# Two blocks in one chip: a delta rule's start reordered between VectorE and GpSimd, a band added by one matmul a head, a gain row fetched through DRAM

## The reference, cut to what matters

```python
def rmsnorm(x, g):
    xf = x.astype(jnp.float32)
    y = xf * lax.rsqrt(jnp.mean(xf * xf, axis=-1, keepdims=True) + EPS)
    return (y * g.astype(jnp.float32)).astype(x.dtype)
...
    return rmsnorm(h, final_norm)          # first model's end, (256, 1024) times a row of 1024 gains
...
# gated delta rule, 6 heads, chunks of 64 tokens (reference form)
lower = jnp.where(strict, jnp.einsum("bhncd,bhnkd->bhnck", kb, k) * decay, 0.0)
sol = lax.linalg.triangular_solve(lower, rhs, left_side=True, lower=True, unit_diagonal=True)
...
# sliding window attention, 12 heads, window 128
s = jnp.where(mask[None, :, None, None], s, -jnp.inf)
m = jnp.maximum(jnp.max(s, axis=-1, keepdims=True), sink)
p = jnp.exp(s - m)
p = (p / (jnp.sum(p, axis=-1, keepdims=True) + jnp.exp(sink - m))).astype(v.dtype)
```

## Time and profile before

| | |
|---|---|
| time, median of 3 runs | 1551.87 us (1551.78 to 1552.45) |
| the profiled execution's own time | 1556.52 us |
| its span | 1554.4 us |
| instructions | 21594 |
| mean granted TensorE clock | 0.997 |
| DMA | 259.77 MB, 167 GB/s |

### The profile page before, as it was taken

The page is one execution under the profiler, slowest core; times in us unless marked ns, Lnnn a source line. Parts: engine busy times, 40 slices in busy tenths (PEclk is TensorE's granted clock), DMA queues, the critical chain, the costliest instruction groups (busy, mean ns, idle before and its releaser), DMA issues.

```text
span 1554.4 us, 21594 instructions
## 1 busy us (share of the span) xinstructions
PE 1530.9 (98%) x8592; PEld 1328.8 (85%) x8592; DVE 599.3 (39%) x992; ACT 842.8 (54%) x1310; POOL 1175.9 (76%) x508
## 2 busy tenths in 40 slices
PE   9999999999999999999999999999999999999997
PEld 7888889999888898888888998988888888888886
DVE  3111017357885712331230697562113737411101
ACT  6444474375656536365463776355444476564543
POOL 8888888888758888478879787517888964388893
PEclk9999999999999999999999999999999999999999
DMA  7556555565544546255556543005555542255562
GB/s 241 185 183 202 165 204 186 173 210 190 192 161 145 195 161 205 96 203 189 189 182 195 196 162 119 28 29 174 190 180 194 194 164 82 94 178 189 189 196 75
DMA packets 71859, 259.77 MB, mean 167 GB/s; under 512 B 7984, under 2 KB 8784, under 8 KB 71504
## 3 DMA queue, kind: packets, MB, share of 16 engines
q1 hardware_dynamic: 69408, 250.44, 48.6%
q10 hardware_dynamic: 2352, 7.96, 1.4%
HBM read 257.29 MB, written 1.08 MB: 166 GB/s over the span
## 4 chain that ended last, share of the span: by engine, by line
PE 89%; DVE 5%; ACT 3%; issue 1%; POOL 1%; DMA 1%; SPq 0%; DVEq 0%; ACTq 0%
PE bank L552 15%; PE bank L554 15%; PE bank L553 15%; PE bank L584 5%; PE bank L582 5%; PE bank L583 5%; PE bank L522 5%; PE bank L524 5%; PE bank L523 5%; PE bank L696 1%; PE bank L1076 1%; PE bank L1097 1%; DMA raw<-in_w 1%; PE bank L668 1%; DVE sq_mem L2028 1%
## 5 line engine op out<-in xcount | busy, mean ns | idle before, releaser
L437 POOL TENSOR_TENSOR w_lo<-raw,w_hi 128x1024 fp32r<-128x1024 f32 x469 | 1130.4, 2443 | 318.4 <-ACT w_hi L1326 318.2
L1326 ACT ACTIVATE w_hi<-raw 128x1024 fp32r<-128x1024 f32 x474 | 487.9, 1058 | 282.1 <-DMA raw<-in_w 278.3
L552 PE MATMUL bank<-w_hi,u_hi 128*128 128x512 f32 x880 | 348.8, 396 | 1.0 <-DVE u_lo L2116 0.6
L554 PE MATMUL bank<-w_hi,u_lo 128*128 128x512 f32 x880 | 343.3, 390 | 0.0
L553 PE MATMUL bank<-w_lo,u_hi 128*128 128x512 f32 x880 | 342.8, 390 | 0.0
L522 PE MATMUL bank<-u_hi,w_hi 128*128 128x256 f32 x688 | 197.0, 286 | 0.0
L552 PEld LDWEIGHTS bank<-w_hi,u_hi 128*128 128x128 f32 x880 | 165.3, 188 | 36.4 <-DVE u_lo L2116 2.1
L554 PEld LDWEIGHTS bank<-w_hi,u_lo 128*128 128x128 f32 x880 | 165.2, 188 | 35.2
L524 PE MATMUL bank<-u_hi,w_lo 128*128 128x256 f32 x688 | 194.7, 283 | 0.0
L523 PE MATMUL bank<-u_lo,w_hi 128*128 128x256 f32 x688 | 194.6, 283 | 0.0
L553 PEld LDWEIGHTS bank<-w_lo,u_hi 128*128 128x128 f32 x880 | 165.4, 188 | 32.6
(11 more groups left out here) (418 smaller groups left out, 2107.6 us busy)
## 6 DMA issues: line engine op xcount, KB each, us to landing
raw<-in_w SPq DMA_DIRECT2D x474, 512.0 KB, 4.4
bc<-acs_scratch ACTq DMA_DIRECT2D x8, 512.0 KB, 5.5
mem_t<-in_mem ACTq DMA_DIRECT2D x2, 1024.0 KB, 6.4
out<-out_t SPq DMA_DIRECT2D x4, 256.0 KB, 2.8
xf<-in_x ACTq DMA_DIRECT2D x1, 512.0 KB, 7.9
xf<-in_x SPq DMA_DIRECT2D x1, 512.0 KB, 8.5
lvl<-in_lvl ACTq DMA_DIRECT2D x1, 448.0 KB, 2.9
band<-in_band ACTq DMA_DIRECT2D x1, 256.0 KB, 6.1
```

Of the source, the lines that this page charges most:

```text
L437: nc.gpsimd.tensor_tensor(w_lo[:, q % RAW, :], raw[:, q % RAW, :], w_hi[:, q % HI, :].bitcast(F32), ALU.subtract).then_inc(split_done, 1)
L552: mm(b[:], hi[:, kt, a], w_hi[:, q % HI:q % HI + 2, c], start=kt == 0, stop=False)
L554: m = mm(b[:], lo[:, kt, a], w_hi[:, q % HI:q % HI + 2, c], start=False, stop=kt == KT - 1)
L1326: fn(w_hi[:, q % HI, :], raw[:, q % RAW, :], ACT.Copy).then_inc(hi_made, 1)
```

## The change

GpSimd's program loses the low part of the last piece of gates ahead of level 1 and gets a wait for both of VectorE's first blocks (`lev_e`) there. In the first round of the loop it waits for `iY` first, then makes that low part and the next one, then level 2. The band is kept as one tile of 384 columns (128 for the first queries, 256 for the second) and added by one matmul a head, and the scores of the twelve masked heads lie next to each other in the bank (`window`). The gains' diagonals, their eight matmuls and two copies go; ScalarE writes the eight columns of gains to DRAM as 1024 single floats after the first feed-forward part, and loads them back, spread over the partitions, behind the second memory's load.

```diff
-SMALL = [("cols", 1), ("xn", 8), ("cb", 4), ("xatt", 8), ("gfin", 2),
+SMALL = [("cols", 1), ("xn", 8), ("cb", 4), ("xatt", 8),
...
-        gdiag = place("gdiag", [P, KT, P], F32, WB + 24)
...
-        band_r = place("band_r", [P, 2, S], F32R, WB + 38)
+        band_r = place("band_r", [P, 384], F32R, WB + 38)
...
+        gain_dram = nc.dram_tensor("gain_scratch", [KT, P], F32).ap()
...
+        def window(b, c):
+
+            return flat(b)[:, c * P:c * P + P * (c + 1)]
...
-            lows(P0["wo0"] - 1, P0["wo0"])
             pool.wait_ge(W["loaded_lvl"], 16)
             pool.wait_ge(unit_free, U0["x0"])
+            pool.wait_ge(W["lev_e"], 2)
...
             level(1)
             for li, lev in enumerate(LEVELS[:-1]):
+                if li == 0:
+                    pool.wait_ge(W["lev_x"], 2)
+                    lows(P0["wo0"] - 1, P0["wo0"])
                 if li < 4:
                     lows(P0["wo0"] + li, P0["wo0"] + li + 1)
-                if li == 0:
-                    pool.wait_ge(W["lev_x"], 2)
                 level(li + 2, lev)
...
-            def gain_and_mem2():
-
-                for n in range(2):
-                    b = start_unit(U0["gfin"] + n)
-                    pe.wait_ge(W["gain_diag"], 1)
-                    for k in range(4):
-                        m = mm(quads(b)[:, k, :], ones[:], gdiag[:, 4 * n + k, :], start=k == 0, stop=k == 3, skip_group_check=True)
-                    m.then_inc(unit_done, 1)
-                mem_sum(1, sq_main, bank[NB])
...
-            ffn(1, ..., late=gain_and_mem2)
+            ffn(1, ..., late=lambda: mem_sum(1, sq_main, bank[NB]))
...
                     if i == 4:
-                        pe.wait_ge(W["band_up"], 2)
+                        pe.wait_ge(W["band_up"], 3)
...
+                    mm(flat(b)[:, 0:384], ident_r[:], band_r[:], start=True, stop=False, skip_group_check=True)
                     for c in range(2):
-                        o, n = b[:, c, 0:P * (c + 1)], P * (c + 1)
-                        mm(o, ident_r[:], band_r[:, c, 0:n], start=True, stop=False)
-                        m = mm(o, q[:, c * P:c * P + P], k[:, 0:n], start=False, stop=True)
+                        m = mm(window(b, c), q[:, c * P:c * P + P], k[:, 0:P * (c + 1)], start=False, stop=c == 1, skip_group_check=True)
...
             ffn(0, first_stats)
+            with nc.allow_non_contiguous_dma(reason="a kilobyte of gains, once"):
+                load(gain_dram.rearrange("k p -> p k"), par[:, PC["final_norm"]:PC["final_norm"] + KT], "gain_out")
...
-            act.wait_ge(unit_done, U0["gfin"])
+            act.wait_ge(unit_done, U0["bacols"])
             load(mem_t[:], mem2_in, "loaded_mem2")
+            act.wait_ge(W["gain_out"], 16)
+            load(gfin[:], gain_dram.rearrange("k p -> (k p)").rearrange("(o n) -> o n", o=1).to_broadcast([P, D]), "gain_in")
...
-                    for n in range(2):
-                        act.wait_ge(unit_done, U0["gfin"] + n + 1)
-                        fn(gfin[:, 512 * n:512 * n + 512], flat(bank_of(U0["gfin"] + n)), ACT.Copy, scale=float(P)).then_inc(unit_free, 1)
                     mem_root(1, rs_mem, bank[NB])
...
-            for kt in range(KT):
-                m = v.tensor_scalar(gdiag[:, kt, :], ident[:], col("final_norm", kt), None, ALU.mult)
-            m.then_inc(W["gain_diag"], 1)
...
-            dve.wait_ge(unit_free, U0["bacols"])
+            dve.wait_ge(W["gain_in"], 16)
...
-                v.tensor_copy(band_r[:], band[:]).then_inc(W["band_up"], 1)
+                v.tensor_copy(band_r[:, 0:P], band[:, 0, 0:P]).then_inc(W["band_up"], 1)
+                v.tensor_copy(band_r[:, P:384], band[:, 1, :]).then_inc(W["band_up"], 1)
...
-                    v.tensor_reduce(stat(0, i)[:, 0:1], b[:, 0, 0:P], AX.X, ALU.max)
-                    v.tensor_reduce(stat(0, i)[:, 1:2], b[:, 1, :], AX.X, ALU.max).then_inc(W["at_row"], 1)
+                    v.tensor_reduce(stat(0, i)[:, 0:1], window(b, 0), AX.X, ALU.max)
+                    v.tensor_reduce(stat(0, i)[:, 1:2], window(b, 1), AX.X, ALU.max).then_inc(W["at_row"], 1)
```

More of the change, by code:

```diff
@@ L308, in build @@
                   "gl_root", "gl_rs", "picks", "pick_zero", "g_step", "gseg", "ex_done", "ex_free", "gexp", "gdecay", "lev_e", "lev_p", "lev_q", "lev_x", "lev_t", "o_eps", "go_ms", "mem_tree", "o_made", "o_used", "go_sq",
-                  "go_sum", "go_root", "go_rs", "go_hi", "rope_tab", "rope_sin", "rope_t", "gain_diag", "out_made", "out_rest",
+                  "go_sum", "go_root", "go_rs", "go_hi", "rope_tab", "rope_sin", "rope_t", "gain_out", "gain_in", "out_made", "out_rest",
                   "out_done"):
@@ L734, in scores @@
                         pe.wait_ge(W["at_exp"], h0 + i - 3)
-                    kind = heads[i]
-                    if kind == "s" and heads[i - 1] != "s":
-                        pe.wait_ge(W["rope_t"], 8)
-                        pe.wait_ge(W["band_up"], 2)
                     for c in range(2):
-                        if kind == "s":
-                            mm(b[:, c, :], ident_r[:], band_r[:, c, :], start=True, stop=False)
                         ks, qs = k_of(i), [q[:, c * P:c * P + P] for q in q_of(i)]
                         for d in range(len(ks)):
-                            m = mm(b[:, c, :], qs[d], ks[d], start=d == 0 and kind != "s", stop=d == len(ks) - 1)
+                            m = mm(b[:, c, :], qs[d], ks[d], start=d == 0, stop=d == len(ks) - 1)
                     m.then_inc(W["at_score"], 1)
@@ L948, in banks_read @@
                 pe.wait_ge(m_sd, 2)
-            ffn(1, lambda s: turn("ffn1", 1) if s == 0 else None, split_ready("ffn1"), banks_read, late=gain_and_mem2)
+            ffn(1, lambda s: turn("ffn1", 1) if s == 0 else None, split_ready("ffn1"), banks_read, late=lambda: mem_sum(1, sq_main, bank[NB]))
             row_stage("mem2k", um_hi, um_lo, lambda kt: pe.wait_ge(mem_lo, 4 + kt // 2 + 1))
@@ L1862, in _ @@
                 for c in range(2):
-                    n = P if i >= 4 and c == 0 else S
-                    m = fn(pr[i % 4][:, c, 0:n], score_banks[i % 3][:, c, 0:n], ACT.Exp, bias=stat(1, i)[:, c:c + 1], scale=0.125,
+                    n, b = P if i >= 4 and c == 0 else S, score_banks[i % 3]
+                    m = fn(pr[i % 4][:, c, 0:n], window(b, c) if i >= 4 else b[:, c, :], ACT.Exp, bias=stat(1, i)[:, c:c + 1], scale=0.125,
                            accum_out=stat(2, i)[:, c:c + 1])
```

## The result

The changed kernel takes 1554.96 us (median of 20 runs, 1553.06 to 1559.25), the kernel before 1551.95 us (20 runs, 1550.63 to 1557.19). The ratio is 1.0023 with a 95% interval of 1.0017 to 1.0029: slower, by 2.6 to 4.5 us. I had forecast 3.0 us less.

A forecast was written before the change was run, and what follows sets the result against it. The prediction took TensorE's work and waits to bound the kernel. Gains of 1.8 (gains), 0.5 (band) and 0.7 (order) sum to 3.0 us, taken from the median 1551.87 to give 1548.9 us, range 1547.2 to 1550.5.

The forecast's parts named there:

- The bottleneck: Whole kernel: TensorE is busy 98% of the span, so a gain must be TensorE work or a TensorE wait removed.
- The order: Delta rule's start, GpSimd: 5.2 us earlier, 1.75 kept after new waits, 0.7 us gained after a slow clock.
- the contention costs 5.2 us: Delta rule's start: VectorE's blocks held up by GpSimd cost TensorE a 3.5 us wait plus 1.7 us of slow clock.
- the new wait: Delta rule's start: TensorE waits 3.0 us for level 2's first block, behind two low parts on GpSimd.
- The later steps: Delta rule's start: VectorE's blocks need 1.9 us, level 1 is hidden, two low parts delay level 2, TensorE waits 3.0 us.
- My second wait of 0.45 us: Delta rule's start: TensorE waits another 0.45 us for level 2's second block, hiding that much of the 1.7 us slow clock.
- Rival 2: Delta rule's start: timed runs before had no slow clock after 974.45, so the order gains nothing; 1549.6 us, chance 0.2.
- The gains: Final norm's gains: eight fp32 matmuls (16 records) leave TensorE, 1.8 us gained, the two DMAs counted at nothing.
- issued where ScalarE idles 2.43 us: Gains' write: ScalarE's idle 2.43 us before it squares x at 192.60 covers the write's issue.
- Rival 3: Gains' write: 1024 four-byte pieces at 0.55 us each, 64 an engine, hold the weights back; slower, 1566 us, chance 0.04.
- some 18 us of lead on the average: Weight supply: pieces issued 26 us ahead need 7.9 us, leaving some 18 us of lead, so it does not bound.
- The band: Twelve masked heads: one 384-column matmul saves 0.09 us a head, six heads count, 0.5 us gained, bounds 0 to 1.8.

The follow-up runs named there:

- the second look at before: The kernel before, unchanged, profiled a second time: 1550.65 us, span 1548.7.
- gains alone, second run: Only the gains' part of the change on the kernel before, repeated on the same chip as the runs with other piece counts: 1550.52 us, ratio 1.0001.
- gains alone, first run: Only the gains' part of the change (DRAM write and load back, eight matmuls gone) on the kernel before: 1552.62 us, ratio 1.0006.
- second level first: The changed kernel with GpSimd making level 2's blocks ahead of the low parts, each low part behind a level: 1551.74 us, ratio 1.0001.
- the order alone: Only GpSimd's new order, with its wait for VectorE's first blocks, on the kernel before: 1555.5 us, ratio 1.0021.
- without the wait for VectorE: GpSimd's new order on the kernel before, less the line waiting on `lev_e`: 1556.85 us, ratio 1.0027.
- the moved write: The changed kernel with the four-byte gains' write moved to just ahead of the cross attention's output projection: 1553.29 us, ratio 1.0011.
- the write in rows: The changed kernel with the 4 KB write made as eight 512-byte rows of the identity, not the right gains: 1553.54 us, ratio 1.0013.

## Why the prediction was wrong

*The bottleneck.* Right: TensorE at 98%, and only its work and its waits count.

*The order, -0.7 us forecast, about +3.3 us measured.* This is the step that failed. "So the contention costs 5.2 us, at that point" was read from one execution, and nine other profiles of that order don't have it, so the 5.2 us that the forecast set against the new wait were not there to be gained. Against the one profile that has them the order did come out near the forecast (0.4 us). The later steps were right: VectorE's blocks took 1.83 us, level 1 was hidden, the two low parts stood ahead of level 2, and the wait there was 2.87 us (forecast 3.0). But there was nothing to set against it. With the old order level 2 starts at 977.60 and is ready before TensorE comes for it. My second wait of 0.45 us did not come, and the clock was on its lower level from 986.3 to 989.8, 1.7 us as forecast, with no wait to hide a part of it. Forecast 3.0 + 0.45 + 1.25 = 4.7, in this profile 2.87 + 1.7 = 4.6. Rows of other kernels show that this clock is not sure: behind the same wait it cost nothing in one and some 3 us in two. Rival 2 had the right suspicion, that the profile's slow clock was not in the timed runs. It did not go far enough: the wait wasn't there either. Two numbers said so. The profiled execution took 1556.52 us and the three timed ones 1551.78 to 1552.45, and I subtracted a gain of the former from the latter. The difference of 4.7 us is almost the 5.2 us of the contention.

*The gains, -1.8 us forecast, +0.9 and +0.2 measured by the ratios (the medians say +1.2 and -0.7).* This is the second step that failed. The 1.8 us were right: in the profiles 1.7 to 2.0 us go at 780. The write, "issued where ScalarE idles 2.43 us", was covered only in its issue; the transfer behind it was counted at nothing, and it makes a wait of 2.2 to 3.0 us on TensorE at 202. Rival 3 had the mechanism (weights held back, a low part late), but took a price per piece and "some 18 us of lead on the average". The pieces leave in 2 us, and at 193 us the lead is far below the average: in before the low part of 199.67 is needed at 202. By the rule of the Trainium skill, DMA: Bandwidth & Descriptors, Specifications, that transfers under 512 bytes become a read-modify-write, the write would be slow for its size; the runs agree in this, 4 KB in four-byte pieces held the weights back and 4 KB in 512-byte rows did not. By what mechanism they did, no run shows.

*The band, -0.5 us forecast, -0.3 in the traces.* The mechanism was right, and what a head saves was mis-sized: 0.055 us, not 0.09. The single step takes 0.26 us as forecast (0.255), but the products behind it take 0.03 us more. Six heads at 0.055 are the 0.3. Over all twelve it is 0.66, of which the longer waits on ScalarE's pr take back 0.2, as the text had it for the other heads.

*The sum.* From the second look at before to the changed kernel the traces give +3.6 (202 to 207 us), -1.7, +4.7 and -0.3: 6.3 us, the difference of the spans 1548.7 and 1555.0. Of these 1.7 us each in the first and the third are slow clock. The ratio says 3.6 and the medians are 3.0 us apart, less than the profiles, since the one profile lies 1.9 us over its median and the other 0.7 under that of its runs. How many executions have each slow stretch is known only as far as the mean clocks above tell. The parts measured alone give, by the ratios, 3.3 + (0.2 to 0.9) + 0.2 = 3.7 to 4.4, which fits the 3.6 within the intervals.

## What to carry to other kernels

Hold the profiled execution's own time against the timed runs before a wait is taken for a cost: where it is several microseconds longer, find out what it has that the others lack, best by a second profile of the same kernel. A transfer in many four-byte pieces belongs where the other queues' loads have lead, as at 630 us here, or its data should be turned so that its rows are 512 bytes. When work is moved behind a wait on one engine, put what the critical engine asks for next first and the filler behind it.

## What the runs showed of the hardware

- Two engines that take turns, and one execution in which they did not. VectorE's operation with two SBUF inputs takes 0.95 us alone, 1.73 and 2.60 beside GpSimd's; GpSimd's takes 1.83 alone and 2.56 beside VectorE's. In the profile shown of before, VectorE started 1.49 us behind GpSimd's low part, in the second look 1.50 us, and yet it stood 7.62 us in the one and 1.73 in the other. The Trainium skill, SBUF — State Buffer, section "SBUF: two separate sides", says that whoever starts first has the shared port pair for the whole instruction and the other blocks. The 1.73 us agree: 0.87 us until GpSimd's low part gives way to its next operation (966.44 to 967.31), then 0.86. The 7.62 us, past the ends of three operations of GpSimd, are not explained by it.
- Whether the granted clock falls behind a wait, and for how long, the length of the wait does not decide. On the low part at 202, a wait of 2.75 us (changed kernel) and one of 2.2 us (gains alone, second run) had 3.4 us at the lower level behind them; 3.0 us (gains alone, first run) and 2.2 us (second level first) had none. On GpSimd's iE the wait was 2.9 us in five kernels: 3.4 us at the lower level in the changed kernel and with the order alone, 6.8 us without the wait for VectorE and with the moved write (it fell inside the wait, and 6 us of it lay behind), none with the write in rows. For the last three, in this order (columns as in the earlier trace rows; 0.72 in 12 us is 12 x 0.28 x 2 = 6.7 us at half clock):

```profile
980.00:992.00 12.00, 9.14 (x56) 8.95 (x55) 2.15 (x5) 3.25 (x6) 11.04 (x7) 0.72 0.01 1
...
980.00:992.00 12.00, 9.24 (x55) 9.22 (x56) 2.16 (x5) 3.48 (x6) 11.02 (x7) 0.72 0.01 1
...
980.00:992.00 12.00, 8.94 (x75) 8.54 (x74) 4.16 (x10) 3.26 (x6) 12.00 (x7) 1.00 0.01 1
```

- The gains' load back, 512 KB read from one 4 KB row for all partitions, lands in 10.0 us, where a piece of weights of that size takes 4.4. It costs nothing here, for its reader comes some 180 us after it has landed.
